# Attention loads of queries and keys: twelve transfers of 320 KB a pair become six of 640 KB

## What is computed

```python
def neighbourhood_attention(q, k, v, rpb):      # 8 heads of 64
    s = einsum('rqhd,rjkhd->hrqjk', q, k[rows near r]) * scale + bias
    p = softmax(s)
    o = einsum('hrqjk,rjkhd->rqhd', p, v[rows near r])
...
h = layer_norm(x) @ w_in                        # q, k, v, recurrence inputs, gates
a_out = neighbourhood_attention(q, k, v, rpb) @ w_branch_na
```

## Time and profile before

| what | value |
|---|---|
| median of 3 runs | 2743.06 us (2741.1 to 2749.04) |
| the profiled execution: its time, its span | 2744.83 us, 2742.7 us |
| PE busy | 2653.2 us, 97% of the span |
| DVE, ACT, POOL busy | 65%, 51%, 21% |
| DMA, mean over the span | 249 GB/s |
| attention stage, up to the first matmul of the recurrence | 471.5 to 591.8 us of the span |

### The profile page before, as it was taken

The page is one execution under the profiler, slowest core; times in us unless marked ns, Lnnn a source line. Parts: engine busy times, 40 slices in busy tenths (PEclk is TensorE's granted clock), DMA queues, the critical chain, the costliest instruction groups (busy, mean ns, idle before and its releaser), DMA issues.

```text
span 2742.7 us, 44087 instructions
## 1 busy us (share of the span) xinstructions
PE 2653.2 (97%) x17944; PEld 2125.6 (77%) x17944; DVE 1792.7 (65%) x2284; ACT 1404.9 (51%) x1801; POOL 563.8 (21%) x513
## 2 busy tenths in 40 slices
PE   9999999889999999997999999999999999999997
PEld 7888888678888878875777777777777777777775
DVE  7211221678899666567776777677767776777788
ACT  3111221668665433324665566556655665666674
POOL 2211110005554333320100110011001100111444
PEclk9999999999999999998999999999999999999999
DMA  7467774796565663455788778877888788878984
GB/s 249 168 199 220 245 254 131 167 304 232 179 222 197 206 228 112 144 199 192 293 295 307 276 289 298 300 282 287 302 292 289 285 305 300 297 281 329 355 318 141
DMA packets 238728, 683.53 MB, mean 249 GB/s; under 512 B 20465, under 2 KB 67064, under 8 KB 233408
## 3 DMA queue, kind: packets, MB, share of 16 engines
q1 hardware_dynamic: 220992, 630.59, 64.7%
q0 software_dynamic: 17536, 50.14, 6.5%
HBM read 576.67 MB, written 103.95 MB: 248 GB/s over the span
## 4 chain that ended last, share of the span: by engine, by line
PE 50%; DVE 1%; DMA 1%; POOL 1%; issue 1%; ACT 0%; POOLq 0%; ACTq 0%; DVEq 0%
PE moe_strip L2591 12%; PE moe_up L2606 4%; PE moe_up L2607 4%; PE moe_up L2608 4%; PE moe_gate L2606 4%; PE moe_gate L2608 4%; PE moe_gate L2607 4%; PE moe_down L2606 4%; PE moe_down L2608 4%; PE moe_down L2607 4%; DMA out<-moe_norm_x 1%; PE moe_turn L2564 0%; PE moe_up L2528 0%; POOL moe_minus_mean L2410 0%; DVE pieces_low L2822 0%
## 5 line engine op out<-in xcount | busy, mean ns | idle before, releaser
L2822 DVE TENSOR_TENSOR pieces_low<-pieces_raw,pieces_high 128x1024 fp32r<-128x1024 f32 x768 | 893.5, 1218 | 348.7 <-PE moe_strip L2591 335.3
L2714 ACT ACTIVATE pieces_high<-pieces_raw 128x1024 fp32r<-128x1024 f32 x768 | 769.3, 1051 | 332.8 <-PE moe_up L2608 195.9
L2591 PE MATMUL moe_strip<-pieces_raw,pieces_xT_p 128*32 128x256 f32 x4096 | 227.9, 380 | 0.5 <-ACT pieces_xT_p L2726 0.5
L2606 PE MATMUL moe_down<-pieces_high,pieces_hdn 128*128 128x512 f32 x512 | 202.8, 396 | 1.8 <-DVE pieces_low L2822 1.8
L2606 PE MATMUL moe_gate<-pieces_high,pieces_xT 128*128 128x512 f32 x512 | 202.4, 395 | 1.4 <-DVE pieces_low L2822 0.7
L2606 PE MATMUL moe_up<-pieces_high,pieces_xT 128*128 128x512 f32 x512 | 202.9, 396 | 0.0
L2591 PEld LDWEIGHTS moe_strip<-pieces_raw,pieces_xT_p 128*32 128x32 f32 x4096 | 129.7, 110 | 93.8 <-issue 10.9
L2608 PE MATMUL moe_gate<-pieces_low,pieces_xT 128*128 128x512 f32 x512 | 199.7, 390 | 0.0
L2607 PE MATMUL moe_up<-pieces_high,pieces_xT 128*128 128x512 f32 x512 | 199.6, 390 | 0.0
L2608 PE MATMUL moe_down<-pieces_low,pieces_hdn 128*128 128x512 f32 x512 | 199.5, 390 | 0.0
L2607 PE MATMUL moe_gate<-pieces_high,pieces_xT 128*128 128x512 f32 x512 | 199.5, 390 | 0.0
(11 more groups left out here) (396 smaller groups left out, 5613.0 us busy)
## 6 DMA issues: line engine op xcount, KB each, us to landing
pieces_raw<-in_w_gate_e SPq DMA_DIRECT2D x128, 1024.0 KB, 5.6
pieces_raw<-in_w_up_e SPq DMA_DIRECT2D x128, 1024.0 KB, 7.2
pieces_raw<-in_w_down_e SPq DMA_DIRECT2D x128, 1024.0 KB, 5.0
bias_fx<-xs SPq DMA_DIRECT2D x40, 1024.0 KB, 5.3
fr_raw<-in_w_in SPq DMA_DIRECT2D x16, 1024.0 KB, 9.2
ws<-fr_late_split SPq DMA_DIRECT2D x32, 512.0 KB, 4.2
bias_fw<-ws SPq DMA_DIRECT2D x32, 512.0 KB, 9.0
mo_gates<-h SPq DMA_DIRECT2D x20, 512.0 KB, 4.4
```

What stands on the lines that cost most here:

```text
L2591: last = nc.tensor.matmul(strip_ps[j * CP:(j + 1) * CP, kind, :], x, raw[g % RAW][:, k * D + j * STRIP:k * D + (j + 1) * STRIP], start=sta ...
L2606: nc.tensor.matmul(to[:], x_k[:, kk, 0:CS], hi, start=(kk == 0), stop=False)
L2714: nc.scalar.activation(high[:, g % HI, cols], raw[g % RAW][:, cols], ACT.Copy).then_inc(hi_done, 1)
L2822: nc.vector.tensor_tensor(low[g % RAW][:, cols], raw[g % RAW][:, cols], high[:, g % HI, cols].bitcast(F32), ALU.subtract).then_inc(lo_done, 1)
```

## The change

`load_heads_of` issues one transfer for each tile and head, over all 128 partitions. For queries, the source takes both halves of `qk` as a leading dimension of 2 (shape 2 x 64 x 1280). For keys, whose two halves are the same rows, the source is 64 x 1280 with a leading broadcast dimension of 2. Each semaphore wait counts 6 transfers in place of 12. Bytes, packets of 5120 bytes, tiles and order of the work stay as they were.

```diff
     for u in range(2):
         head = slice((2 * hp + u) * NA_DIM, (2 * hp + u + 1) * NA_DIM)
-        for half in range(2):
-            part = slice(half * NA_DIM, (half + 1) * NA_DIM)
-            sp.dma_start(q[part, u, :].bitcast(F32), qk[0, half, head, :]).then_inc(done, 16)
-            sp.dma_start(k_hi[part, u, :].bitcast(F32), qk[1, 0, head, :]).then_inc(done, 16)
-            sp.dma_start(k_lo[part, u, :].bitcast(F32), qk[1, 1, head, :]).then_inc(done, 16)
+        sp.dma_start(q[:, u, :].bitcast(F32), qk[0, :, head, :]).then_inc(done, 16)
+        for half, k in enumerate((k_hi, k_lo)):
+            sp.dma_start(k[:, u, :].bitcast(F32), qk[1, half, head, :].unsqueeze(0).to_broadcast([2, NA_DIM, T]))\
+              .then_inc(done, 16)
...
-                        pool.wait_ge(pair_in, 16 * 12)
+                        pool.wait_ge(pair_in, 16 * 6)
...
-                        pe.wait_ge(pair_in, 16 * 12)
+                        pe.wait_ge(pair_in, 16 * 6)
...
-                        pe.wait_ge(loaded[w], 16 * 12 * ((hp + 1) // 2))
+                        pe.wait_ge(loaded[w], 16 * 6 * ((hp + 1) // 2))
```

More of the change, by code:

```diff
@@ L773, in _ @@
                     if hp == 0:
-                        pool.wait_ge(pair_in, 16 * 12)
+                        pool.wait_ge(pair_in, 16 * 6)
                     else:
-                        pool.wait_ge(loaded[w], 16 * 12 * ((hp + 1) // 2))
+                        pool.wait_ge(loaded[w], 16 * 6 * ((hp + 1) // 2))
                     if hp >= 2:
```

## The result

The changed kernel takes 2950.2 us (median of 4, 2948.67 to 2959.2), against 2742.08 us before (median of 4): the ratio is 1.0767, 95% interval 1.075 to 1.0784. The forecast was 2963 us with a range of 2915 to 3020. The profiled execution took 2950.76 us, its span is 2947.5, 204.8 us longer than before.

What follows compares the result with a forecast made beforehand. PE, busy 97% of the span, bounds the kernel, so its waits for loads count in full. Front stage 47 plus pairs 1 to 3 at 57.6, 58.0 and 57.8 make 220 us: 2963 us, range 2915 to 3020.

Steps and rivals of the forecast that it cites:

- the ring of load and next issue: Attention stage: a load lands, 8.75 us later the next is issued; load cost above 16 us is paid three times.
- How many engines: SP's new loads: engines must divide both slowest dimensions, 2 and 128, so two of 16 work; two near 25 GB/s: 84%.
- the 43.7% of POOL's queue: Queue share at 140 to 144 us, beside a store of `padded`, read as seven engines of 16 (43.75%).
- Price of a load: A pair's 3.93 MB on two engines at 24.1 to 25.4 GB/s each: 80 us a load, against 22.
- the 3 us for start and landing: Added to a load's data time, taken from a 256 KB store that lands 3.7 us after issue, 0.6 us its data.
- the 407 GB/s of the prediction's row: Upper rate of all 16 engines on transfers of 128 rows before the change, 25.4 GB/s for one engine.
- Front stage: Stores of `hT` wait behind pair 0's loads, PE behind the stores; attention starts at 518.6 instead of 471.5 us: +47 us.
- the upper end of its range: 3020 us: loads at 81.5 us (+16), and SP held at its issues by full queues, 10 us a load at most (+40).
- Behind pair 3: Remaining transfers, 11.8 MB or 29 us, fit in the 30.7 us before the recurrence: 0, or a few us.
- All 16 engines, faster: Rival: loads of about 13 us on all engines, the three PE waits vanish, 2725 us; chance 8%.

Runs made afterwards that it cites:

- e1_interleaved: The changed kernel's six transfers a pair, with the two halves as the inner dimension of the source: 2722.77 us, ratio 0.9933 to the kernel before.
- e7_twelve_of_128_rows: Layout of `e1_interleaved`, each of its six transfers cut in two by tokens: twelve transfers of 128 rows of 2560 bytes; 2716.03 us.
- e8_every_second: Layout of `e1_interleaved`, filled by the earlier kernel's twelve transfers of 64 rows, each writing every second partition instead of one half: 2728.41 us.
- e4_first_pair_old: The changed kernel, but pair 0, loaded in the front stage, keeps the twelve transfers of before: 2905.99 us, 44 below the changed kernel.

## Why the prediction was right

**What bounds the stage.** Right: the ring of load and next issue. From release to next issue it is now 8.3 and 8.2 us (597.15 to 605.42, 682.64 to 690.84), for 8.75 before. Its other half: the waits vanish once a load is at 16 us or less (loads of 12.4 to 16.1 us in `e1_interleaved`, `e7_twelve_of_128_rows`, `e8_every_second`).

**How many engines.** Right, and it decided the case: 12.7% of 16 is two engines. The evidence from the trace of before was weaker than the prediction took it to be: the 43.7% of POOL's queue lies so near to 7/16 by the choice of the window. Its two halves, 140 to 142 and 142 to 144 us, give

```profile
q0 software_dynamic: 49, 0.08, 49.6%
q0 software_dynamic: 67, 0.09, 37.8%
```

and all of 138 to 148 us gives 35.0%. Beside another of the eight stores, from 263 to 265 us, it is 62.3%, well above the 43.75% of seven engines, so other transfers of that queue are in the share. The row could not count engines; that its reading came true is luck, as far as that row goes. What counts them are the runs: the Trainium skill's rule on the largest divisor (DMA: Bandwidth & Descriptors, Why a DMA increments its semaphore by 16 and not by 1) holds on SP's queue for 2, 4, 8 and 16 (shares of 0.13, 0.26, 0.56 and 1.02).

**Price of a load.** 80 us against 77.0 to 77.4: the two engines move 53 GB/s, not 50.8, so the data takes 74 us, and the 3 us for start and landing hold. An engine has 26 GB/s with all sixteen at work too (421 GB/s in `e1_interleaved`); the 407 GB/s of the prediction's row was a little low. Three times the difference is 8 us too much.

**Front stage.** +47 against +43.2. The chain was as forecast: unit 7's copy on DVE waited 64.4 us for the landing of a store of `hT`, PE 40.5 us for the copy, and the last unit ran at half clock (0.50 granted from 507 to 512 us, behind the 40.5 us in which PE did nothing; 506.74 us to its copy at 512.26, 5.5 us, 5.6 in the forecast). One link was wrong: the prediction let the nine stores be issued from 436 us and only their sixteenths lie behind the loads. In truth SP itself was held at the issues of the loads until 468.31 us; the prediction has that only at the upper end of its range. The landing came at 506 us for the forecast 510, so the price is nearly the same. `e4_first_pair_old` put it at 43 to 44 us by itself.

**Behind pair 3.** 30.6 us to the recurrence, 30.7 before: nothing, as forecast.

**Sum.** 220 us forecast, 207.0 at the start of the recurrence and 204.8 at the end. Of the 13 us, 8 are the price of the loads, 4 the front stage and 1 the time from release to next issue.

**Rivals.** All 16 engines, faster, at 2725 us: it did not happen here, but its working is confirmed by the run in which it does, 2722.77 us. The change's aim was sound; the order of two dimensions in the source turned 18 us of gain into 208 us of loss.

## What to carry to other kernels

Ahead of fusing transfers, look at the slowest dimension of source and target of each: the largest number up to 16 that divides both was the number of DMA engines that worked in every form tried here (2, 4, 8 and 16). A leading dimension of 2, by a stride or by a broadcast, leaves two. Put the small dimension inside and permute the partitions, wherever only their sum matters. A load that shows all engines busy at half the rate may be written to half of the partitions: spread the target. Twelve transfers in place of six then cost up to 4 us a load here, and PE waited for none of them.

## What was not expected of the hardware

- **A transfer on two engines also blocks the engine that issues it.** The first two issues of pair 1's load took 0.51 us each, the third 10.33, the fourth and fifth 12.12 each (as the one at 439.56 us above), about the 12.4 us in which two engines move 640 KB:

```profile
520.72 0.51 SPq L679 DMA_DIRECT2D na_k_hi<-qk  x1
521.27 10.33 SPq L679 DMA_DIRECT2D na_k_lo<-qk  x1
531.64 12.12 SPq L677 DMA_DIRECT2D na_q<-qk  x1
543.80 12.12 SPq L679 DMA_DIRECT2D na_k_hi<-qk  x1
```

The same six issues took 0.60 to 0.71 us each when sixteen engines carried them (`e1_interleaved`). Everything behind on SP's queue waits with the load: the stores of the front stage, and the values `na_v`. No run shows what limit the third issue met.
- **Halving the engines need not halve the rate.** Four engines moved 102 GB/s, eight 136 to 138 in two loads and 200 to 220 in the other two, sixteen 214 to 221, all in transfers of 64 rows to one half of the partitions.
